# RWKV sample chunk moved to second place, its products and updates reshaped, scores, gates and tokens placed between levels, and the mLSTM sample update in 32-row halves

## The reference

```python
# mLSTM, last chunk: every sample sequence has a state of its own
C_new = dec * C + einsum('bhs,bhsv,bhsd->bhvd', wl, v, k)   # and n likewise
# RWKV, per token
sa = einsum('bhvk,bhk->bhv', S, -kk)
S = S * w + sa[..., None] * (kk * a) + v[..., None] * k
y = einsum('bhvk,bhk->bhv', S, r)
# then head norm, weights ln_r_g and ln_r_b, the bonus sum(r*k*r_k)*v, and a gate
```

## Time and profile before

| | us |
|---|---|
| median of 3 runs (1894.75 to 1896.31) | 1895.19 |
| the profiled execution | 1895.57 |
| its span, first to last instruction | 1893.8 |
| PE busy, x15094 | 1712.1 (90%) |
| DVE busy, x1518 | 1063.2 (56%) |
| POOL busy, x743 | 888.2 (47%) |
| ACT busy, x638 | 456.8 (24%) |
| mean granted TensorE clock | 0.924 |

### The profile page before, as it was taken

The page is one execution under the profiler, slowest core; times in us unless marked ns, Lnnn a source line. Parts: engine busy times, 40 slices in busy tenths (PEclk is TensorE's granted clock), DMA queues, the critical chain, the costliest instruction groups (busy, mean ns, idle before and its releaser), DMA issues. The chain is left out here.

```text
span 1893.8 us, 35704 instructions
## 1 busy us (share of the span) xinstructions
PE 1712.1 (90%) x15094; PEld 1632.2 (86%) x15094; DVE 1063.2 (56%) x1518; ACT 456.8 (24%) x638; POOL 888.2 (47%) x743
## 2 busy tenths in 40 slices
PE   6999888647989689999998999898899999998996
PEld 5999866527888489999998999897689999998996
DVE  4817633576553467777764123967747777766012
ACT  4001100243111223333332003112233333332001
POOL 4667797622000145444445765650056444445673
PEclk8999876668997789999998999998899999999998
DMA  4222201104200113222222222117422222222222
GB/s 164 78 78 88 102 1 50 45 1 135 78 3 6 45 46 96 78 82 84 78 89 64 81 82 74 67 55 223 148 71 86 79 87 78 86 80 63 82 81 89
DMA packets 50104, 146.75 MB, mean 77 GB/s; under 512 B 17488, under 2 KB 19168, under 8 KB 47840
## 3 DMA queue, kind: packets, MB, share of 16 engines
q1 hardware_dynamic: 50016, 145.55, 24.7%
HBM read 125.22 MB, written 19.13 MB: 76 GB/s over the span
## 5 line engine op out<-in xcount | busy, mean ns | idle before, releaser
L279 PE MATMUL PP<-arena_r,dual_r 128*128 128x288 f32 (+1 forms) x6428 | 1114.5, 298 | 45.0 <-DVE arena_r L266 16.0
L279 PEld LDWEIGHTS PP<-arena_r,dual_r 128*128 128x128 f32 (+1 forms) x6428 | 964.4, 190 | 48.7 <-issue 25.9
L279 PE MATMUL PP<-hT_r,dual_r 128*128 128x288 f32 (+1 forms) x2176 | 645.5, 297 | 0.0
L266 POOL TENSOR_TENSOR dual_r<-w_ring,dual_r 128x1024 fp32r<-128x1024 f32 (+1 forms) x198 | 484.3, 2446 | 18.0 <-ACT dual_r L1840 4.6
L266 POOL TENSOR_TENSOR dual_r<-w_ring,cst 128x1024 fp32r<-128x1024 f32 (+1 forms) x114 | 216.2, 1896 | 549.3 <-PE PP L279 262.3
L279 PEld LDWEIGHTS PP<-hT_r,dual_r 128*128 128x128 f32 (+1 forms) x2176 | 408.8, 188 | 1.2
L269 DVE SCALAR_TENSOR_TENSOR rowbuf<-rowbuf,convp 128x592 f32<-128x592 f32 x176 | 271.2, 1541 | 91.4 <-ACT rowbuf L1863 90.7
L279 PE MATMUL PP<-arena 64*64 64x64 f32 (+6 forms) x3704 | 220.3, 249 | 20.2 <-DVE arena L2352 5.2
L279 PEld LDWEIGHTS PP<-arena 64*64 64x64 f32 (+2 forms) x3704 | 198.1, 148 | 40.0 <-issue 14.0
L266 DVE TENSOR_TENSOR xT<-PP,xT 128x576 f32<-128x576 f32 x32 | 24.2, 757 | 261.2 <-PE PP L279 261.2
L1840 ACT ACTIVATE dual_r<-w_ring 128x1024 fp32r<-128x1024 f32 x84 | 89.2, 1062 | 332.2 <-PE PP L279 332.2
(11 more groups left out here) (257 smaller groups left out, 1445.3 us busy)
## 6 DMA issues: line engine op xcount, KB each, us to landing
w_ring<-in_w SPq DMA_DIRECT2D x150, 512.0 KB, 3.6
w_ring<-in_w_down SPq DMA_DIRECT2D x32, 448.0 KB, 3.3
w_ring<-in_w_down SPq DMA_DIRECT2D x16, 512.0 KB, 3.5
xT<-in_x SPq DMA_DIRECT2D x4, 576.0 KB, 7.0
gy_scratch<-dual SPq DMA_DIRECT2D x1, 2304.0 KB, 13.0
dual<-gy_scratch SPq DMA_DIRECT2D x1, 2304.0 KB, 14.1
out_y<-hT SPq DMA_DIRECT2D x4, 576.0 KB
hT<-in_C SPq DMA_DIRECT2D x1, 2064.0 KB, 7.8
```

What stands on the lines that cost most here:

```text
L266: return eng.tensor_tensor(out, a, b, op)
L279: return nc.tensor.matmul(out, lhsT, rhs, start=start, stop=stop)
```

## The change

`ORDER` puts the sample chunk (`NCR`) second; counters that were computed from the chunk number now come from its place in `ORDER` (`LB` levels before, `R1N` r1 evacuations, `NST` states). For ordinary chunks the next chunk's scores and gates are placed two tiles after level 3 and two after level 4, and its tokens after level 5; behind the sample's levels, and in the iteration that carries the sample's sequence, the scores stay together. The last level but one no longer computes and copies a product that nothing reads. The sample products take both halves of `AR` at once (16 columns, row halves in turn); a second copy `RT` holds the output part, which the identity adds to `y`. The sample updates are 32-row matmuls of 256 columns on masked rows for four sequences (`sample_rows`, `sample_states`, `sample_add`). The bonus matmuls stand between the last chunk's sequence parts, and ScalarE adds `ln_r_b`. The mLSTM update uses two 32-row halves per pair of sequences, eight groups of four matmuls, three in PSUM. Two waits for the eleven adds become waits for eight (L639, L1250).

```diff
-        Km = dring[0:64, 0:4096].rearrange("p (h j n) -> p h j n", h=4, j=8)
+        Km = dring[0:64, 0:2048].rearrange("p (h j n) -> p h j n", h=4, j=4)
+        KM_PAIR = (3, 0, 1)
...
-        UVm = dring[:, 0:4096].rearrange("p (a q j n) -> p a q j n", a=2, q=4, j=8)
+        UVm = at(9216 + 12 * T, 2, 4, 4, 64)
+        RT = at(9216 + 12 * T + 2048, 4, 64)
+        seqhalf_all = c_("seqh", 4)
+        ORDER = (0, NCR, *range(1, NCR))
+        AT_S = ORDER.index(NCR)
+        TOP = [5 if c < NCR else 2 for c in ORDER]
+        LB = [sum(t + 1 for t in TOP[:i]) for i in range(NCR + 2)]
+        R1N = [i + 1 + (i >= AT_S) for i in range(NCR + 1)]
+        NST = [sum(c < NCR for c in ORDER[:i]) for i in range(NCR + 2)]
...
+            sp.wait_ge(S("rs_st"), 1)
+            sp.dma_start(o["sS"], SS).then_inc(S("sS_written"), 16)
             sp.wait_ge(S("rk_st"), NCR + 1)
             out("pS", Sr)
-            sp.wait_ge(S("rs_st"), 1)
-            sp.dma_start(o["sS"], SS).then_inc(S("sS_written"), 16)
...
+                        for g in range(8):
+                            if g >= 3:
+                                pe.wait_ge(S("ml_sst"), g - 2)
+                            h, j0 = g // 2, 2 * (g % 2)
+                            for j in range(2):
+                                for a in range(2):
+                                    q = slice(32 * a, 32 * a + 32)
+                                    last = mm(PP[KM_PAIR[g % 3]][:, a, 129 * j:129 * j + 129], Km[q, h, j0 + j, :],
+                                              vaug[q, h, :])
...
-                def scores(c):
+                def scores(i, ps):
+                    c = ORDER[i]
                     cols = slice(LR * c, LR * c + LR)
...
+                    for p in ps:
+                        if i == 0:
+                            pe.wait_ge(S("rw_prep"), p + 1)
+                            pe.wait_ge(S("rw_pool"), p + 1)
+                        if 4 * i + p >= 2:
+                            pe.wait_ge(S("rk_g"), 4 * i + p - 1)
+                        if i > AT_S + 1 and p == 0:
+                            pe.wait_ge(S("rs_sc"), 2)
...
-                                if k < top:
+                                if k < top - 1:
                                     mm(b[r, 0:128], v[:, 2, :], v[:, 0:2, :])
-                                    last = mm(b[r, 128:192], v[:, 0, :], v[:, 2, :])
                                 else:
                                     last = mm(b[r, 64:128], v[:, 2, :], v[:, 1, :])
+                                if k < top:
+                                    last = mm(b[r, 128:192], v[:, 0, :], v[:, 2, :])
...
-                            for r in rows2():
-                                for j in range(8):
+                            for j in range(8):
+                                for r in rows2():
                                     e = SEQ + 8 * j
-                                    last = mm(bank(5)[r, 64 * p + 8 * j:64 * p + 8 * j + 8], SS[r, p, j, :],
-                                              AR[r, p, 0, e:e + 8])
+                                    out = bank(5)[r, 128 * p:128 * p + 128].rearrange("p (a n) -> p a n", a=2)
+                                    last = mm(out[:, :, 8 * j:8 * j + 8], SS[r, p, j, :], AR[r, p, :, e:e + 8])
                         last.then_inc(S("rk_r1"), 1)
-                        pe.wait_ge(S("rk_r1c"), NCR + 1)
-                    elif c:
-                        pe.wait_ge(S("rk_uc"), c)
+                        pe.wait_ge(S("rk_r1c"), R1N[i] - 1)
...
+                                last = mm(out, ident[r, r], RT[r, p, :], False, True)
...
+                def sample_states(q):
+                    g = AT_S % 2
+                    pe.wait_ge(S("rk_g"), 4 * AT_S + 8)
+                    pe.wait_ge(S("e_samples"), 3 + q)
+                    if q:
+                        pe.wait_ge(S("rs_sc"), q)
+                    for pp in range(2):
+                        p = 2 * q + pp
+                        for k in range(2):
+                            for h in range(2):
+                                for a in range(2):
+                                    r, w = slice(64 * h, 64 * h + 64), slice(64 * h + 32 * a, 64 * h + 32 * a + 32)
+                                    last = mm(PP[0][r, a, 256 * pp:256 * pp + 256], tok[w, g, p, k, :],
+                                              UVm[w, k, p, :, :].rearrange("p j n -> p (j n)"), k == 0, k == 1)
+                    last.then_inc(S("rs_s"), 1)
+                def bonus(p):
+                    if p >= 2:
+                        pe.wait_ge(S("rw_bonusc"), p - 1)
+                    for a in range(2):
+                        last = mm(PP[p % 2][:, a, 0:TH], headones, rkp[:, p, a * TH:(a + 1) * TH])
+                    last.then_inc(S("rw_bonus"), 1)
+                scores(0, range(RP))
+                pe.wait_ge(S("s5_evac"), 10)
+                tokens(0)
+                for i in range(NCR + 1):
+                    after = i < NCR
+                    level(i, 0)
+                    if i:
+                        seq_r1(i - 1)
+                    level(i, 1)
+                    if i:
+                        seq_u(i - 1)
+                    level(i, 2)
+                    if i:
+                        seq_ys(i - 1)
+                    if TOP[i] == 5:
                         for k in (3, 4, 5):
-                            level(c, k)
+                            level(i, k)
+                            if i == AT_S + 1:
+                                if k < 5:
+                                    sample_states(k - 3)
+                            elif after and k < 5:
+                                scores(i + 1, (2 * k - 6, 2 * k - 5))
+                    if after:
+                        if TOP[i] != 5 or i == AT_S + 1:
+                            scores(i + 1, range(RP))
+                        tokens(i + 1)
+                for q in range(2):
+                    pe.wait_ge(S(f"rk_lc{q}"), LB[NCR + 1])
                 seq_r1(NCR)
+                bonus(0)
+                bonus(1)
                 seq_u(NCR)
+                bonus(2)
+                bonus(3)
                 seq_ys(NCR)
                 pe.wait_ge(S("rk_yc"), NCR + 1)
...
+                pe.wait_ge(S("rk_st"), NCR + 1)
...
+                if i == AT_S:
+                    act.wait_ge(S("rk_r1"), R1N[i] - 1)
+                    both_ = bank(5).rearrange("p (a k b) -> p a k b", a=4, k=2)
+                    A(QT, both_[:, :, 0, :], ACT.Copy)
+                    A(RT, both_[:, :, 1, :], ACT.Copy).then_inc(S("rk_r1c"), 1)
...
+                if i == AT_S + 1:
+                    act.wait_ge(S("e_samples"), 4)
...
             r1_copy(NCR)
+            for p in range(2):
+                act.wait_ge(S("rw_bonusc"), p + 1)
+                A(rkp[:, p, :], rkp[:, p, :], ACT.Identity, bias=v_("ln_r_b", p)).then_inc(S("rw_gatec"), 1)
             u_copy(NCR)
+            for p in range(2, 4):
+                act.wait_ge(S("rw_bonusc"), p + 1)
+                A(rkp[:, p, :], rkp[:, p, :], ACT.Identity, bias=v_("ln_r_b", p)).then_inc(S("rw_gatec"), 1)
             y_copy(NCR)
...
-                            e0, e1 = 3 * g, min(3 * g + 3, 32)
+                        for g in range(8):
+                            h, j0 = g // 2, 2 * (g % 2)
                             dve.wait_ge(S("ml_supd"), g + 1)
-                            tt(V, Csf[:, e0:e1, :], Csf[:, e0:e1, :], bank(6 + g % 2)[:, 0:129 * (e1 - e0)].rearrange(
-                                "p (a b) -> p a b", b=129), ALU.add).then_inc(S("ml_sst"), 1)
+                            x = Cs[:, h].rearrange("p (a j) n -> p a (j n)", a=2)[:, :, 129 * j0:129 * j0 + 258]
+                            tt(V, x, x, PP[KM_PAIR[g % 3]][:, :, 0:258], ALU.add).then_inc(S("ml_sst"), 1)
...
+                            part = slice(0, 3, 2) if k < top - 1 else slice(2, 3)
+                            last = V.tensor_copy(new[:, :, part, :], b[:, :, part, :])
...
+                def sample_rows(q):
+                    dve.wait_ge(S("rk_uc"), AT_S + 1)
+                    for p in (2 * q, 2 * q + 1):
+                        tt(V, UVm[:, 0, p], bc(U[:, p, :], 1, 4), bc(seqhalf_all, 2, 64), ALU.mult)
+                        last = tt(V, UVm[:, 1, p], bc(tok[:, AT_S % 2, p, 2, :], 1, 4), bc(seqhalf_all, 2, 64), ALU.mult)
+                    last.then_inc(S("e_samples"), 1)
+                def sample_add(q):
+                    dve.wait_ge(S("rs_s"), q + 1)
+                    x = SS[:, 2 * q:2 * q + 2].rearrange("p b (a j) n -> p b a (j n)", a=2)
+                    tt(V, x, x, PP[0].rearrange("p a (b n) -> p b a n", b=2), ALU.add).then_inc(S("rs_sc"), 1)
+                gate(0, range(RP))
+                for i in range(NCR + 1):
+                    after, sampled = i < NCR, i == AT_S + 1
                     for k in range(3):
...
```

(80 more changed lines are left out.)

165 lines of the change are left out of this document (72 added, 93 removed).

## The result

The changed kernel takes 1840.06 us (median of four runs, 1838.41 to 1841.14) against 1895.24 beside it: ratio 0.9707 (95% interval 0.9694 to 0.9721), 55.2 us less. The forecast was 1840.6.

The account below looks back on a forecast made before the run. TensorE was taken to bound the mLSTM adds and nearly fill the prompt chunks, with a serial tail behind them. Gains of 6.4 (mLSTM), 46.7 (RWKV stage) and 1.9 (head norm) make 55.0: 1895.6 to 1840.6 us, range 1830 to 1858.

Parts of the forecast that it names:

- mLSTM: mLSTM sample update: 32-row matmuls run two abreast, 0.86 us a group, so the last add ends 6.4 us earlier.
- First chunk: First RWKV prompt chunk, level 0 to the next level 0, with a shorter first edge: 12.7 us.
- chunks 2 to 6: Five RWKV prompt chunks with scores and gates between the levels, 5 x 14.86 us instead of 17.5 each.
- 1 for the splits: GpSimd's first two e_out splits move into chunk 2 and slow VectorE there: 1 us, bounds 0 and 4.
- Sample chunk: Sample chunk placed second: its levels with chunk 0's sequence, then scores, gates and tokens undivided, 12.0 us.
- Chunk 1: Prompt chunk that carries the sample's sequence (products, copies, rows, two matmul sets, adds): 26.0 us against 14.9.
- 4 for the clock: TensorE's clock falls to 1.2 GHz around chunk 1's sample products: 4 us added, bounds 0 and about 8.
- the alternation gains little at 1.2 GHz: Sample products alternating between row halves: 0.14 us each against 0.158 before, both at 1.2 GHz.
- Last chunk: Chunk 7, now ending the stage, from level 0 to level 5: 11.2 us.
- end: Behind chunk 7's level 5: r1, bonuses, u, outputs, state matmuls, state add and copies' waits, 9.0 us.
- Head norm: Head norm's first matmuls run at 2.4 GHz after a dense end, not at 0.50: 1.9 us gained.
- 150.2: Forecast RWKV stage: 145.2 us of chunks and end, plus 4 for the clock and 1 for splits, against 196.9.

Follow-up runs that it names:

- the last experiment: Changed kernel with one of the four bonus sums moved from the end to behind the sample products, where TensorE waits for ScalarE's copies: 1836.74 us (0.9687).
- The third experiment: Changed kernel with the sample chunk last again, all the rest of the change kept: 1838.29 us (0.9701).

## Why the prediction was right, and where its terms were off

- *mLSTM* 6.4, measured 6.47: two abreast, 0.86 us a group, the add 0.69, all as estimated. The Trainium skill's TensorEngine Tiling (Array Packing), section Tiling Modes, says that a change of tiling mode drains TensorE. No idle time is seen at one here: the sets of 32-row pieces, between 64-row levels, take 2.0 us each at a clock of 1.00 (the trace models where a matmul ends, so a short drain could hide in it). The rows from which 2.2 was priced stand between such changes too, at a granted clock of 0.85, which the reading left out.
- *First chunk* 12.7, measured 12.61; *chunks 2 to 6* 74.3 and 1 for the splits, measured 75.80 (494.84 to 570.64), 1.07 of it in chunk 2. There the second add of level 0, of two operands in SBUF, took 1.53 us beside GpSimd's splits instead of 0.29. TensorE's queue is the bound, as argued: in the whole stage it waits 10.9 us, 5.1 of it for the token copy.
- *Sample chunk* 12.0, measured 12.51.
- *Chunk 1* 26.0 and 4 for the clock, measured 26.79. The clock fell as foreseen, but for 3 us, and cost 1.6 (the last experiment). The rest is 25.2: products 4.0 instead of 4.3, sets 2.0 instead of 2.2. The 26.0 is not a plain sum: the items listed for it come to 28.3 without RT's saving, and which 2.3 of them hide was not written down, so it was met as a whole and not term by term. The Trainium skill's TensorE: Matmul & The Clock Gate, section The mechanism of Part 3, lets a weight load overlap a running matmul only on other row groups; the trace agrees (73 records in three us on one half, 110 in turn, at one clock). My sentence that the alternation gains little at 1.2 GHz was not put to a test by itself.
- *Last chunk* 11.2 and *end* 9.0, measured 11.71 (570.64 to 582.35, the end of level 5's last add) and 9.95. The copy of U stands behind two biases, 585.68 to 587.26, as said; the end was priced 1 us short.
- *Head norm* 1.9, measured 1.91.

So 0.5 us too little three times and 0.95 once, and 3.2 too much in chunk 1, make 149.37 of 150.2. Each term's mechanism is seen in the trace, but not that the move is what pays (below). That the whole time came within 0.6 us is partly luck: the misses cancel, and the same kernel run again has a median of 1837.50.

What the sum did not ask is which edit pays. I priced the old tail as work that the move hides beside other chunks. The third experiment shows that it need not be hidden: with the old order and the new pieces the gain is the same. It lies in the tail's pieces and the clock under them (29.5 us from the sample chunk's level 0 to the head norm: shorter products, outputs and updates, bias and scaling no longer in front of the head norm) and at the edges (12.7). TensorE is busy in 138 of the stage's 149 us, so there is little idle time beside the other chunks for the sample's work to fill. The other way round, the move with the old pieces, was not run.

## What to carry to other kernels

Where the tail of a stage is serial, ask first whether its pieces are badly cut (rows in one group, columns too few, a slow partner engine beside them), and only then whether it can be moved: here, with the pieces cut well, the place made no difference, since the engine that they need was busy in either. Behind many small matmuls the clock can fall, and what follows then takes longer than the wait that is seen; independent work of full width put into that wait kept the clock here and paid more than the wait's length. When executions vary by more than the effect, compare a stage of the trace that starts and ends on the same two instructions, and take from an untouched part of it how far it varies by itself. Look at a mean of a few instructions one by one, with the clock beside each: the biases' 1.80 us and half of the two sets' 11.0 were means of unlike ones.

## What the runs showed of the hardware

- A VectorE tensor-scalar of 576 columns takes 0.51 to 0.54 us alone and 2.03 to 2.48 beside GpSimd's splits of 1.89 to 2.44; adds that read PSUM kept their 0.29 us beside them.
- 64 products of 64 rows and 16 columns: 4.0 us with the halves in turn, 7.0 with one half at a time, of which the last 2 ran at 1.2 GHz.
- TensorE's clock fell to 1.2 GHz while it was busy without a pause, in such products on one half (at 470.39, products from 465.42 to 472.39) and with the halves in turn (at 472.97, products from 469.20 to 473.33, scores undivided).
- Sixteen 32-row matmuls of 256 columns at 2.4 GHz: 2.0 us going round four groups, 4.7 with four in a row on one.
